# Main operand buffers begin at multiples of 1024 bytes

## What is computed

```python
def swiglu(x, wi, wo):
    gate, up = jnp.split(x @ wi, 2, axis=-1)
    return (jax.nn.silu(gate) * up) @ wo
...
for li in range(2):                      # first block
    h = h + 0.5 * swiglu(rms_norm(h, ffn1_norm[li]), ffn1_wi[li], ffn1_wo[li])
    hn = rms_norm(h, mix_norm[li])
    h = h + (gla_pool_mixer(hn, ...) if li == 0 else dsa_mixer(hn, ...))
    h = h + 0.5 * swiglu(rms_norm(h, ffn2_norm[li]), ffn2_wi[li], ffn2_wo[li])
x = rms_norm(h, final_norm)
...                                      # second block, one layer: the same frame, with
x = x + mixed @ w_o                      # a mixer of two attentions (mla and fox) with gates
```

## Time and profile before

| | |
|---|---|
| median of three runs | 1511.88 us (1511.41 to 1513.79) |
| profiled execution | 1513.46 us |
| its span | 1511.7 us |
| TensorE busy | 1481.7 us, 98% |
| VectorE busy | 876.1 us, 58% |
| ScalarE busy | 709.9 us, 47% |
| GpSimd busy | 84.6 us, 6% |
| mean granted TensorE clock | 0.993 |
| read from memory | 263.52 MB |

### The profile page before, as it was taken

One profiled execution on the slowest core, in us unless ns is written; L12 is line 12 of the kernel. 1 busy time (PEld: TensorE's weight loads), 2 busy tenths in 40 slices (PEclk: granted clock), 3 DMA queues, 4 the chain that ended last, 5 costly groups with the idle time before them and its releaser, 6 DMA issues.

```text
span 1511.7 us, 16927 instructions
## 1 busy us (share of the span) xinstructions
PE 1481.7 (98%) x7061; PEld 1231.4 (81%) x7061; DVE 876.1 (58%) x1040; ACT 709.9 (47%) x836; POOL 84.6 (6%) x101
## 2 busy tenths in 40 slices
PE   8999999999999999999899999999999889999999
PEld 6888888888888888887688888888888768888887
DVE  6465456665546555469665554754547787765543
ACT  6444355644444444444554444544346666354432
POOL 0000003000000000006000000000000440000000
PEclk9999999999999999999999999999999999999999
DMA  9655463465545655463365555555556352555552
GB/s 317 218 189 171 151 209 113 139 220 176 189 167 190 200 194 175 159 188 126 111 206 173 192 173 189 195 195 175 181 174 202 118 168 84 195 187 187 183 181 70
DMA packets 144946, 265.66 MB, mean 176 GB/s; under 512 B 7102, under 2 KB 27030, under 8 KB 144614
## 3 DMA queue, kind: packets, MB, share of 16 engines
q1 hardware_dynamic: 143030, 259.11, 52.1%
q0 software_dynamic: 1104, 4.35, 0.9%
q10 hardware_dynamic: 736, 1.12, 0.2%
HBM read 263.52 MB, written 1.05 MB: 175 GB/s over the span
## 4 chain that ended last, share of the span: by engine, by line
PE 90%; DVE 7%; ACT 2%; POOL 1%; issue 1%; POOLq 0%; DVEq 0%; ACTq 0%
PE ps L529 28%; PE ps L531 28%; PE ps L530 28%; PE ps L558 2%; DVE wlo L1479 2%; PE ps L541 1%; PE ps L716 1%; PE ps L916 1%; PE ps L656 1%; POOL m_qf L2104 0%; PE ps L1052 0%; DVE d_i L1811 0%; PE ps L622 0%; DVE d_m L1807 0%; DVE d_mx L1682 0%
## 5 line engine op out<-in xcount | busy, mean ns | idle before, releaser
L1479 DVE TENSOR_TENSOR wlo<-raw,whi 128x2048 fp32r<-128x2048 f32 (+4 forms) x268 | 568.6, 2127 | 422.6 <-ACT whi L1092 422.4
L1092 ACT CAST whi<-raw 128x2048 fp32r<-128x2048 f32 (+4 forms) x268 | 473.5, 1770 | 447.3 <-PE ps L531 446.2
L529 PE MATMUL ps<-whi,xt_hi 128*128 128x512 f32 (+3 forms) x1376 | 533.7, 388 | 5.2 <-DVE wlo L1479 5.1
L531 PE MATMUL ps<-whi,xt_lo 128*128 128x512 f32 (+3 forms) x1376 | 527.3, 383 | 0.0
L530 PE MATMUL ps<-wlo,xt_hi 128*128 128x512 f32 (+3 forms) x1376 | 526.6, 383 | 0.0
L529 PEld LDWEIGHTS ps<-whi,xt_hi 128*128 128x128 f32 x1376 | 258.5, 188 | 56.5 <-issue 4.3
L531 PEld LDWEIGHTS ps<-whi,xt_lo 128*128 128x128 f32 x1376 | 258.4, 188 | 50.9
L530 PEld LDWEIGHTS ps<-wlo,xt_hi 128*128 128x128 f32 x1376 | 258.7, 188 | 48.0
L529 PE MATMUL ps<-whi,yt_hi 128*128 128x512 f32 (+3 forms) x108 | 43.5, 403 | 9.0 <-DVE wlo L1479 6.9
L1118 ACT ACTIVATE junk<-X 128x512 f32<-128x512 f32 x40 | 25.4, 634 | 43.4 <-DVE X L1534 40.0
L531 PE MATMUL ps<-whi,yt_lo 128*128 128x512 f32 (+3 forms) x108 | 42.0, 389 | 0.0
(11 more groups left out here) (381 smaller groups left out, 1588.4 us busy)
## 6 DMA issues: line engine op xcount, KB each, us to landing
raw<-in_ffn_wi SPq DMA_DIRECT2D x79, 1024.0 KB, 5.2
raw<-in_ffn_wo SPq DMA_DIRECT2D x40, 1024.0 KB, 5.0
raw<-in_ffn_w_gate SPq DMA_DIRECT2D x20, 1024.0 KB, 5.0
raw<-in_ffn_w_up SPq DMA_DIRECT2D x20, 1024.0 KB, 5.0
raw<-in_ffn_w_down SPq DMA_DIRECT2D x20, 1024.0 KB, 5.0
raw<-in_w_in SPq DMA_DIRECT2D x14, 1024.0 KB, 5.2
raw<-in_ffn_wi SPq DMA_DIRECT2D x16, 512.0 KB, 4.7
raw<-in_even_w_in SPq DMA_DIRECT2D x6, 1024.0 KB, 5.2
```

Of the source, the lines that this page charges most:

```text
L529: e.matmul(o, h, hi_w, start=i == 0 and j == 0, stop=False)
L531: t = e.matmul(o, l, hi_w, start=False, stop=end and j == nk - 1)
L1092: e.copy(whi[0:n, v % SPLIT, c], raw[0:n, v % RAW, c]).then_inc(s_hi.mark(*[(v, j) for j in js]), 1)
L1479: e.tensor_tensor(wlo[0:n, v % SPLIT, c], raw[0:n, v % RAW, c], whi[0:n, v % SPLIT, c].bitcast(F32), ALU.subtract).then_inc(s_lo.mark(*[(v ...
```

## The change

Two things are done. `ident`, `nv`, `na` and `nb`, 896 bytes together, are allocated ahead of `raw` instead of behind `yt_lo`. Two buffers that nothing uses, `whole` (384 bytes, after `trig`) and `whole1` (320 bytes, after `r_`), fill up to the next round address ahead of the stages' own buffers. In the mla stage `FT` and `kr_room` have no buffers of their own any more but lie in parts of `mat.P1`. Instructions and waits are as they were, in their order; their addresses differ, and `FT` is a view with a step between its two rows.

```diff
+        ident = sb("ident", [128, 128])
+        nv = sb("nv", [128, 32])
+        na = sb("na", [128, 32])
+        nb = sb("nb", [128, 32])
         raw = sb("raw", [128, RAW, 2048])
         whi = sb("whi", [128, SPLIT, 2048], F32R)
         wlo = sb("wlo", [128, SPLIT, 2048], F32R)
         X = sb("X", [128, 2, D])
         XT = Turned(sb("xt_hi", [128, 8, 256], F32R), sb("xt_lo", [128, 8, 256], F32R))
         YT = Turned(sb("yt_hi", [128, 8, 256], F32R), sb("yt_lo", [128, 8, 256], F32R))
-        ident = sb("ident", [128, 128])
         G = sb("G", [128, 128])
         junk = sb("junk", [128, 512])
         ssq = sb("ssq", [128, 2, 2])
-        nv = sb("nv", [128, 32])
-        na = sb("na", [128, 32])
-        nb = sb("nb", [128, 32])
         ny = sb("ny", [128, 32])
...
         trig = sb("trig", [128, 2, 3, 80])
+        whole = sb("whole", [128, 96])
...
         r_ = sb("r_", [128, 2, 80], F32, early)
+        whole1 = sb("whole1", [128, 80], F32, early)
...
-            FT = sb("m_ft", [128, 2, 80], F32, sc)
...
-            kr_room = [sb("m_kr1", [128, 32], F32, sc), sb("m_kr2", [128, 32], F32, sc)]
             q_room = [LAT[:, 0, 0:256], LAT[:, 1, 0:256]]
             mat = Attention("m_", lambda n, s: sb(n, s, F32, sc), (FQ[:, :, :].rearrange("p b n -> p (b n)"), FK[:, 0, :]))
+            kr_room = [mat.P1[:, 0, 0:32], mat.P1[:, 0, 32:64]]
+            FT = mat.P1[:, 1:3, 0:80]
```

## The result

The changed kernel takes 1510.30 us in the median of 21 runs (1509.32 to 1512.44). The kernel before, in 21 runs on the same chip, takes 1512.31 (1511.12 to 1514.63). The ratio is 0.9984, with an interval of 0.9978 to 0.9990: 2.0 us less by the medians, 2.4 by the ratio, where 0.5 was forecast. That is under 0.2%, but the interval leaves out 1: a small gain, clear of the noise of these runs.

A forecast was written before the change was run, and what follows sets the result against it. TensorE's matmuls were taken to bound the kernel. Profiled 1513.46 us minus 0.5 for a1, everything else 0, gave 1512.9; from the runs' median, 1511.88 - 0.5 = 1511.4 us, range 1504.5 to 1515.

The forecast's parts named there:

- What bounds the kernel: Whole kernel: TensorE paces it, busy 1481.7 of 1511.7 us; loads and splits run ahead.
- Loads, splits and the borrowed room in mla: Weight loads, ScalarE and VectorE splits, `FT` and `kr_room` in `P1`: each 0; bounds 0.3 us for loads, 0.6 for splits.
- a1's 264 matmuls, 0.5 us: Down projection of feed-forward layer a1: tiles moved from 320 to 0 save 0.5 us, bounds 0 and 0.6.
- The 5466 others, 0: Large matmuls outside a1's down projection: no change expected from their new start addresses; at best 80 us faster.
- The rule on two read ports: Weight load and moving operand read through independent ports, so no distance could matter; a1's term would be 0, not 0.5.
- Rival A: Large matmuls: common start at 0 removes per-step start-up, 1428 to 1491 us; 0.14 together with a clock lapse gone.
- The 14.7 ns: Part of each 226.7 ns step of a 512-column matmul that is not columns, at 0.414 ns a column.
- Rival B: Large matmuls: common start makes TensorE's two reads meet, 7 ns per three, 13.5 us slower, 1525 us; chance 0.07.
- The clock: Three stretches at 1.2 GHz in the mixers: up to 8 us could come or go; main width of the forecast.

The follow-up runs named there:

- experiment 2: Kernel before plus 64 unused bytes ahead of a1's buffers, putting its hidden tiles at 384 instead of 320 modulo 1024: 1511.98 us, ratio 0.9995.
- Experiment 1: Kernel before with only `ident`, `nv`, `na` and `nb` moved ahead of `raw`, stage buffers left where they were: 1521.40 us, ratio 1.0067.
- the scan: Changed kernel with hidden tiles spaced a few bytes further apart, so one run shows many distances from the weights: 1518.24 us, one run.
- experiment 4: Changed kernel plus 64 unused bytes between `X` and `xt_hi`, so every large stationary tile lies 64 bytes on: 1544.19 us, ratio 1.0220.
- Experiment 12: Changed kernel with the four transposes of b1's last flip done three times, so the dsa stage is reached later: 1512.77 us, ratio 1.0004.
- experiments 1 to 5: Besides those listed here singly, the third: changed kernel without `whole1`, a1's hidden tiles at 704 modulo 1024: 1511.33 us, ratio 0.9997.
- experiment 8: Changed kernel plus 64 unused bytes ahead of `ident`, every buffer 64 further on and all distances kept: 1510.42 us, ratio 0.9987.
- experiment 9: Changed kernel with only the 256-column blocks laid 192 bytes into their slots of `raw`, `whi` and `wlo`: 1510.05 us, ratio 0.9985.
- experiment 10: Changed kernel with `ident` last of the four small buffers, at 0 modulo 256 instead of 128: 1510.52 us, ratio 0.9984.
- experiment 11: Changed kernel with 64 unused bytes on each side of `ident`, which begins at 192 modulo 256: 1511.55 us, ratio 0.9989.
- experiment 6: Changed kernel timed once more, nothing altered, against the kernel before on the same chip: 1510.44 us, ratio 0.9985.

## Why the prediction was right, and where it wasn't

*What bounds the kernel.* Right: the large waits of the other engines moved by 1 us at most, and every term found lies in TensorE's steps or its clock. Loads, splits and the borrowed room in mla are the zeros they were taken for, as far as 0.1 us in a stretch can show; in the mla stage behind 1182 us, where the lapses lie, so small a term could hide.

*a1's 264 matmuls, 0.5 us.* The size is right: 0.52 in the trace, 0.54 in experiment 2 with nothing else changed. The reason given was wrong. "At 0 the distance modulo 128 becomes that of the other layers" chose the one of two readings that the rows of before allowed equally; 192 is 64 modulo 128 and 192 modulo 256. Experiment 1 refutes the first by 10 us. That the forecast did not suffer was luck: this change brings all these distances to 0 modulo 512, where both readings say the same.

*The 5466 others, 0.* Right for their settled steps. What failed is that this term counted only settled steps, and the small matmuls were not in the sum at all. The transposes read `ident`, whose distance to `X` and `H` the change does alter, and the large matmuls behind them then settle sooner: 0.6 us, as much as a1. The hint stood in the earlier trace rows: one of the starts shown there has 0.40 where the others have 0.39, because it is one of the steps behind a transpose that have not settled.

*The rule on two read ports.* The Trainium skill ("TensorE: Matmul & The Clock Gate", Step-by-step: what each phase is for) was weighed with the words "The row speaks against the rule in that strict form". The runs speak against it far more strongly: 64 bytes of distance on all stationary tiles cost 32 us. That it is the two reads that meet is an inference; the runs show only that the step depends on the distance, for which the strict form leaves no room.

*Rival A.* Refuted by the change itself and, for the distances tried, by the scan: 227 ns is the least. The 14.7 ns themselves came from comparing with 256-column matmuls, which stood at a distance that is poor for them. At 64 bytes most of these step 113 or 114 ns, half of 226.7, so that hardly anything is left of the 14.7 ns that could be called a start-up. The Trainium skill's figure of 216 ns (the same page, Back-to-back issue gap) is reached by no distance tried, for these operands.

*Rival B.* It did not happen, since distance 0 is the best place and not the worst. But what it feared, a price on every large matmul by the distance, is real, and its price of 7 ns per three matmuls was too low for most distances: experiment 4 shows some 20 ns per three (3 x 6.6) at 64. The 7 ns belong to the distance of 192.

*The clock.* The forecast gave lapses as width and none to the centre, and that width, 7 us down, is why 1510.30 lies in the range; the centre, 1511.4, had a quarter of the gain. The profile's 2.83 us at 723 us belongs to one execution, not to the change; what belongs to it is that the runs with a lower clock become rarer. At equal clock (0.994) the changed kernel is about 1.0 us ahead in the mean of the runs (1511.7 against 1510.7), near the 1.1 us of the steps; the rest is the mixture of runs. It has two parts. The runs at 0.993 or below went from 53 of 116 to 3 of 32, and at 2.4 us each that is 0.9 us. The runs at 0.995 went from 2 of 95 (those of before with a clock on record) to 14 of 32, worth some 0.3 us; the profiles at 0.995 and above lack the short lapse near 12 us that all those at 0.994 have, and what makes it rarer no run shows. Experiment 12 supports that the first part follows the arrival in the dsa stage, in a sample of 11 runs; it isn't shown beyond that. If it holds, some 0.9 us of the gain hang on where the stages happen to fall and would be lost with the next edit that shifts them by a microsecond.

## What to carry to other kernels

Where TensorE paces a kernel with 512-column fp32r matmuls, look at the distance between the stationary tile and the moving operand, not at where either starts: in this kernel a multiple of 256 bytes gave 227 ns a step, most other distances 229 to 235, and a careless 64 bytes cost 2%. Matmuls of 256 columns had another best distance, and the place of the small operand of the transposes mattered too, by a rule that stays open; both are worth trying one by one. And before a few microseconds are read off a pair of profiles, sort many runs of both kernels by their granted clock, and compare at equal clock.

## What the runs showed of the hardware

- The step of an fp32r matmul of 512 columns depends on the distance of its two operands with a period of 256 bytes: 227 ns at 0, 256 and 512, 229 at 192, 232 at 128, 233 at 64 (experiments 1 to 5). Moving all starts by 64 bytes with the distances kept changes nothing (experiment 8).
- At 256 columns it is the other way round: distance 0 gives 120 ns, 64 bytes apart gives 113 or 114 in most steps (experiment 4), and so does -192, the same modulo 256 (experiment 9; in duration 283 and 278 ns).
- After a transpose the large matmuls take 3 to 10 steps to settle to 227 ns, and how many depends on where the transpose's `ident` lies (experiment 10), though not by its distance modulo 256 alone (experiment 11).
- The same program ran in 1509.1 to 1512.5 us, with mean granted clocks from 0.995 to 0.993 (experiment 6 and the result). The share of runs with a mean clock of 0.993 or below, which in the profiles goes with a lapse in the dsa stage, was 53 of 116 before and 3 of 32 with an arrival 0.8 us earlier, and 5 of 11 with the arrival put back (experiment 12, a small sample).
